# A fused encoder layer with 32 experts on one core: the order of TensorE's work in the expert pass, the third token tile as 128 rows, and the gate's activation in halves

## The reference

```
logits = xt @ w_router + b_router            # 320 tokens, 32 experts
top 4 experts of each token, gates = softmax over the 4
for each block of rows of one expert e:
    gu   = x_rows @ w_gate_up[e] + b_gate_up[e]        # 1024 -> 2048
    gate = minimum(gu[:, :1024], 7);  up = clip(gu[:, 1024:], -7, 7)
    act  = (up + 1) * gate * sigmoid(1.702 * gate)
    y    = act @ w_down[e] + b_down[e]                 # 1024 -> 1024
out[token] += gate_of_token * y
y_prompt, y_sample = rms_norm(x + out) * norm_final_g
```

## Time and profile before

| what | value |
|---|---|
| median of 3 runs | 1284.58 us (1284.41 to 1285.18) |
| the profiled execution | 1285.43 us, span 1283.7 us |
| TensorE | busy 1243.4 us, 97% |
| VectorE, ScalarE | busy 39% and 16% |
| HBM traffic | 436.33 MB, 340 GB/s over the span |
| granted TensorE clock | 0.996 |

### The profile page before, as it was taken

The page is one execution under the profiler, slowest core; times in us unless marked ns, Lnnn a source line. Parts: engine busy times, 40 slices in busy tenths (PEclk is TensorE's granted clock), DMA queues, the critical chain, the costliest instruction groups (busy, mean ns, idle before and its releaser), DMA issues.

```text
span 1283.7 us, 17240 instructions
## 1 busy us (share of the span) xinstructions
PE 1243.4 (97%) x6406; PEld 542.4 (42%) x6407; DVE 497.1 (39%) x996; ACT 207.6 (16%) x407; POOL 37.6 (3%) x64
## 2 busy tenths in 40 slices
PE   6999999999999999999999999999999999999996
PEld 5655754664333343333333334333334333333332
DVE  2643645457433333333323334233333233233334
ACT  1131224452100111001101001010011100011102
POOL 2000002400000000000000000000000000000000
PEclk9999999999999999999999999999999999999998
DMA  9623125238999969999987999996999999699995
GB/s 323 219 80 118 66 89 194 72 134 315 419 430 427 428 271 428 429 427 427 427 380 323 427 428 427 427 428 289 417 427 428 428 426 426 276 431 426 426 426 202
DMA packets 48010, 436.33 MB, mean 340 GB/s; under 512 B 6229, under 2 KB 7373, under 8 KB 19318
## 3 DMA queue, kind: packets, MB, share of 16 engines
q1 hardware_dynamic: 43984, 429.41, 80.5%
q0 software_dynamic: 2080, 6.48, 1.5%
q10 hardware_dynamic: 1926, 0.18, 0.1%
HBM read 432.33 MB, written 3.72 MB: 340 GB/s over the span
## 4 chain that ended last, share of the span: by engine, by line
PE 82%; DMA 13%; DVE 2%; issue 1%; ACT 1%; POOL 0%; ACTq 0%; SPq 0%; DVEq 0%; POOLq 0%
PE PS L1848 34%; PE PS L1888 17%; DMA ring<-in_w_gate_up_dram 12%; PE PS L1339 6%; PE PS L1348 5%; PE PS L1806 5%; PE PS L1294 4%; PE PS L1774 4%; PE PS L1350 1%; DMA dsk<-in_d_skip_dram 1%; PE PS L1642 1%; PE PS L1831 1%; PE PS L1616 1%; PE PS L1500 1%; PE PS L1503 0%
## 5 line engine op out<-in xcount | busy, mean ns | idle before, releaser
L1848 PE MATMUL PS<-ring,r 128*64 128x512 f32 x2304 | 520.0, 596 | 11.9 <-DMA ring<-in_w_gate_up_dram 11.3
L1848 PEld LDWEIGHTS PS<-ring,r 128*64 128x64 f32 x2304 | 158.6, 137 | 314.9 <-issue 281.1
L1888 PE MATMUL PS<-ring,r 128*64 128x512 f32 x1152 | 255.1, 595 | 0.3
L1163 DVE SCALAR_TENSOR_TENSOR r<-PS,gprev,r 128x512 f32<-128x512 f32 (+1 forms) x222 | 152.4, 741 | 113.6 <-PE PS L1806 112.1
L1888 PEld LDWEIGHTS PS<-ring,r 128*64 128x64 f32 x1152 | 82.2, 137 | 148.4 <-issue 146.2
L1266 DVE TENSOR_TENSOR yy<-PS,yy 128x512 fp32r<-128x512 f32 x36 | 24.9, 692 | 249.8 <-ACT yy L747 249.8
L736 ACT ACTIVATE r<-r 128x512 f32<-128x512 f32 x36 | 22.7, 629 | 504.9 <-DVE r L1249 504.9
L1249 DVE TENSOR_SCALAR r<-PS 128x512 f32<-128x512 f32 x36 | 24.9, 692 | 202.6 <-PE PS L1848 202.6
L1339 PE MATMUL PS<-r,ring 128*128 128x323 f32 x320 | 91.3, 442 | 2.1 <-ACT r L523 2.1
L1294 PE MATMUL PS<-ident,r 128*128 128x128 f32 (+5 forms) x490 | 80.6, 295 | 10.7 <-DVE r L782 9.9
L1294 PEld LDWEIGHTS PS<-ident,r 128*128 128x128 f32 (+5 forms) x490 | 61.5, 183 | 35.6 <-issue 17.6
(11 more groups left out here) (321 smaller groups left out, 742.4 us busy)
## 6 DMA issues: line engine op xcount, KB each, us to landing
ring<-in_w_gate_up_dram SPq DMA_DIRECT2D x96, 2048.0 KB, 16.3
ring<-in_w_down_dram SPq DMA_DIRECT2D x64, 2048.0 KB, 16.7
ring<-in_w_gate_up_dram SPq DMA_DIRECT2D x64, 1024.0 KB, 16.4
ring<-in_w_in_dram SPq DMA_DIRECT2D x8, 2048.0 KB, 14.8
ring<-in_w_out_dram SPq DMA_DIRECT2D x3, 2048.0 KB, 7.5
r<-in_x_prompt_dram SPq DMA_DIRECT2D x2, 512.0 KB, 3.9
r<-in_x_prompt_dram POOLq DMA_DIRECT2D x2, 512.0 KB, 4.4
out_dram<-r POOLq DMA_DIRECT2D x2, 512.0 KB, 5.5
```

Of the source, the lines that this page charges most:

```text
L1163: v.scalar_tensor_tensor(xx, PS[0:rows, out_banks(t)[h], :], gprev[0:rows, t:t + 1], xx, ALU.mult, ALU.add)\
L1848: last = mm(PS[64 * h:64 * h + 64, m, :], xt[:, k % 4, k // 4, :], w[:, kk, D * m + 512 * h:D * m + 512 * h + 512], start=False, stop=(k = ...
L1888: last = mm(PS[64 * h:64 * h + 64, 2, :], at[:, kk, c, :], w[:, kk, 512 * h:512 * h + 512], start=(c == 0 and kk == 0), stop=(c == 1 and k ...
```

## The change

Seven things are changed. On TensorE `gather` moves from behind the up products to a place ahead of chunk 3. `combine` at its old place does tile 0 alone, tiles 1 and 2 (`combine_rest`) come behind the last up product. Then follow `turn`, `places` and, last before the down products, the transposes of `ac`. The third tile of `x` holds its 64 tokens as 128 rows of 512 columns: the upper half of the columns is moved to partitions 64 to 127. Its output is one product of 128 rows for each part in place of two pairs, and one sum in place of two. The sigmoid and what feeds it and follows it run in two halves of 256 columns. The copy of bank 5 becomes four: tile 0 early, tile 1 and two blocks of 64 x 64 behind `combine_rest`. In the tail the products with the high part go ahead of the low part, into five banks. The third tile is scaled as 512 columns and written by two transfers, for which the last gain is also loaded in halves.

```
 SyncE
-            sp.dma_start(y_sample[0, :, :], xn[0:SS, 2, :]).then_inc(s["y_out"], 16)
-            sp.wait_ge(s["y_out"], 48)
+            for h in range(2):
+                sp.dma_start(y_sample[0, :, 512 * h:512 * h + 512], xn[64 * h:64 * h + 64, 2, 0:HALF]).then_inc(s["y_out"], 16)
+            sp.wait_ge(s["y_out"], 4 * 16)
 GpSimd
+            for h in range(2):
+                pool.dma_start(gfin_halves[64 * h:64 * h + 64], ... .to_broadcast([64, HALF])).then_inc(s["gfin_in"], 16)
 ScalarE
-            a.activation(place[:, 0:TC], PS[:, 4, 0:TC], ACT.Copy).then_inc(s["c_ready"], 1)
+            a.activation(place[:, 0:256], PS[:, 4, 0:256], ACT.Copy)
+            for h in range(2):
+                last = a.activation(place[64 * h:64 * h + 64, 256 + 64 * h:320 + 64 * h], PS[64 * h:64 * h + 64, 4, 256:TC], ACT.Copy)
+            last.then_inc(s["c_ready"], 1)
+            a.activation(x[64:128, 2, 0:HALF], x[0:SS, 2, HALF:D], ACT.Copy).then_inc(s["rows_split"], 1)
             def expert_pass(b):
-                act.wait_ge(s["g_ready"], b + 1)
-                a.activation(sg, ug, ACT.Sigmoid, scale=ALPHA).then_inc(s["sig_ready"], 1)
                 act.wait_ge(s["ct_mm"], b + 1)
-                act.wait_ge(s["comb_mm"], 6 * b + 6)
-                a.activation(place[:, :], PS[:, 5, 0:128 * NT], ACT.Copy).then_inc(s["c_ready"], 1)
+                act.wait_ge(s["comb_mm"], 5 * b + 2)
+                a.activation(place[:, 0:128], PS[:, 5, 0:128], ACT.Copy)
                 act.wait_ge(s["xe_mm"], b + 2)
                 a.activation(xe, bank(3), ACT.Copy).then_inc(s["xe_ev"], 1)
+                for q in range(2):
+                    part = slice(256 * q, 256 * q + 256)
+                    act.wait_ge(s["g_ready"], 2 * b + q + 1)
+                    a.activation(sg[:, part], ug[:, part], ACT.Sigmoid, scale=ALPHA).then_inc(s["sig_ready"], 1)
+                act.wait_ge(s["comb_mm"], 5 * b + 5)
+                a.activation(place[:, 128:256], PS[:, 5, 128:256], ACT.Copy)
+                for h in range(2):
+                    at0 = 256 + 64 * h
+                    last = a.activation(place[64 * h:64 * h + 64, at0:at0 + 64], PS[64 * h:64 * h + 64, 5, at0:at0 + 64], ACT.Copy)
+                last.then_inc(s["c_ready"], 1)
 VectorE
-                accumulate(6 * b, 0)
-                accumulate(6 * b, 1)
+                accumulate(5 * b, range(1), OUT_BANKS)
...
-                v.tensor_scalar(ug, bank(0), LIMIT, None, ALU.min).then_inc(s["g_ready"], 1)
-                dve.wait_ge(s["sig_ready"], b + 1)
-                v.tensor_tensor(sg, sg, ug, ALU.mult).then_inc(s["glu_ready"], 1)
+                for q in range(2):
+                    part = slice(256 * q, 256 * q + 256)
+                    v.tensor_scalar(ug[:, part], bank(0)[:, part], LIMIT, None, ALU.min).then_inc(s["g_ready"], 1)
+                for q in range(2):
+                    part = slice(256 * q, 256 * q + 256)
+                    dve.wait_ge(s["sig_ready"], 2 * b + q + 1)
+                    dve.wait_ge(s["g_ready"], 2 * b + 2)
+                    v.tensor_tensor(sg[:, part], sg[:, part], ug[:, part], ALU.mult).then_inc(s["glu_ready"], 1)
...
-                accumulate(6 * b, 2)
+                gathered(b + 1)
+                accumulate(5 * b, range(1, NT), OUT_BANKS)
...
-                gathered(b + 1)
 TensorE
+            def combine_rest(b):
+                pe.wait_ge(s["o_ev"], 5 * (b + 1) + 4)
+                for part in range(2):
+                    spread(1, part, OUT_BANKS)
+                pe.wait_ge(s["g_ready"], 2 * (b + 1) + 2)
+                for part in range(2):
+                    spread(2, part, OUT_BANKS)
+            def combine_last(b):
+                pe.wait_ge(s["c_ready"], b + 2)
+                pe.wait_ge(s["o_ev"], 5 * (b + 1) + 2)
+                for part in range(2):
+                    pe.wait_ge(s[("yy_ready", "yyl_ready")[part]], b + 2)
+                    for t in range(NT):
+                        spread(t, part, LAST_BANKS)
 in expert_pass
                     if c == outputs:
-                        combine(b - 1, 0)
-                        combine(b - 1, 1)
+                        combine(b - 1)
+                    if c == GU_CHUNKS - 1:
+                        if beside:
+                            gather_first(1)
+                        else:
+                            gather(b + 1)
...
                         last.then_inc(s["gate_mm"], 1)
-                        combine(b - 1, 2)
                         for kk in range(2):
                             last = gate_up(kk, 1)
                         last.then_inc(s["gu_mm"], 1)
-                if beside:
-                    gather_first(1)
-                else:
-                    gather(b + 1)
+                combine_rest(b - 1)
+                turn(b + 1)
+                pe.wait_ge(s["c_ready"], b + 2)
+                places(b + 1)
                 pe.wait_ge(s["act_ready"], b + 1)
                 pe.wait_ge(s["at_ev"], b + 1)
                 for c in range(4):
                     last = tr(PS[:, 4, 128 * c:128 * c + 128], every_fourth(ac, c))
                 last.then_inc(s["at_mm"], 1)
-                pe.wait_ge(s["c_ready"], b + 2)
-                places(b + 1)
-                turn(b + 1)
                 pe.wait_ge(s["at_ev"], b + 2)
-def out_banks(t):
-    return ((6, 7), (2, 4), (6, 7))[t]
+OUT_BANKS = (6, 7, 6, 7, 0)
+LAST_BANKS = (6, 7, 0, 1, 5)
```

More of the change, by code:

```diff
@@ L206, in build @@
         gfin = view(r2, 512, D)
+        gfin_halves = view(r2, 0, HALF)
         lgp = (view(r2, 1024, 128), view(r2, 1152, 128), view(r2, 1280, SS))
@@ L756, in _ @@
             a.activation(stat[:, 11:12], stat[:, 10:11], ACT.Sqrt)
[L757 to L762, removed]
+            for t in range(2):
+                act.wait_ge(s["o_ev"], 5 * total + 2 * t + 4)
+                step(a.activation(r6[:, 0:D], x[:, t, :], ACT.Square, accum_out=stat[:, t:t + 1]))
+                a.activation(stat[:, 3 + t:4 + t], stat[:, t:t + 1], ACT.Sqrt,
+                             scale=1.0 / D, bias=stat[:, 10:11]).then_inc(s["sqrt4"], 1)
+            act.wait_ge(s["o_ev"], 5 * total + 7)
+            step(a.activation(r6[:, 0:HALF], x[:, 2, 0:HALF], ACT.Square, accum_out=stat[:, 2:3]))
+            for h in range(2):
+                other = slice(64 - 64 * h, 128 - 64 * h)
+                last = a.activation(stat[64 * h:64 * h + 64, 12:13], stat[other, 2:3], ACT.Identity,
+                                    scale=1.0 / D, bias=stat[other, 10:11])
+            step(last)
+            a.activation(stat[:, 5:6], stat[:, 2:3], ACT.Sqrt, scale=1.0 / D, bias=stat[:, 12:13]).then_inc(s["sqrt4"], 1)
         @block.vector
@@ L1100, in _ @@
             add_att(3)
-            step(v.memset(place[:, TC:128 * NT].bitcast(f32), 0.0))
+            step(v.memset(place[:, 256:128 * NT].bitcast(f32), 0.0))
             step(v.memset(zeros32, 0.0))
@@ L1156, in gathered, with accumulate @@
                                 ALU.mult).then_inc(s["xt_ev"], 1)
[L1158 to L1164, removed]
+            def accumulate(n, tiles, banks):
+                for t in tiles:
+                    for h in range(2 if t < 2 else 1):
+                        dve.wait_ge(s["comb_mm"], n + 2 * t + h + 1)
+                        xx = x[:, t, 512 * h:512 * h + 512]
+                        v.scalar_tensor_tensor(xx, bank(banks[2 * t + h]), gprev[:, t:t + 1], xx, ALU.mult, ALU.add)\
+                            .then_inc(s["o_ev"], 1)
             positions_of(0, 0)
@@ L1239, in expert_pass @@
                 dve.wait_ge(s["gates_held"], b + 2)
-                accumulate(6 * b, 0)
-                accumulate(6 * b, 1)
+                if first:
+                    dve.wait_ge(s["rows_split"], 1)
+                accumulate(5 * b, range(1), OUT_BANKS)
                 dve.wait_ge(s["ct_mm"], b + 1)
@@ L1275, in _ @@
             dve.wait_ge(s["gates_held"], total + 2)
+            accumulate(5 * total, range(NT), LAST_BANKS)
+            dve.wait_ge(s["gfin_in"], 3 * 16)
             for t in range(NT):
[L1277 to L1281, removed]
                 dve.wait_ge(s["sqrt4"], t + 1)
-                step(v.reciprocal(stat[0:rows, 6 + t:7 + t], stat[0:rows, 3 + t:4 + t]))
-                v.scalar_tensor_tensor(xn[0:rows, t, :], x[0:rows, t, :], stat[0:rows, 6 + t:7 + t],
-                                       gfin[0:rows], ALU.mult, ALU.mult).then_inc(s["fin_ready"], 1)
+                step(v.reciprocal(stat[:, 6 + t:7 + t], stat[:, 3 + t:4 + t]))
+                if t < 2:
+                    v.scalar_tensor_tensor(xn[:, t, :], x[:, t, :], stat[:, 6 + t:7 + t], gfin, ALU.mult, ALU.mult)\
+                        .then_inc(s["fin_ready"], 1)
+                else:
+                    v.scalar_tensor_tensor(xn[:, t, 0:HALF], x[:, t, 0:HALF], stat[:, 6 + t:7 + t], gfin_halves, ALU.mult, ALU.mult)\
```

(32 more changed lines are left out.)

20 lines of the change are left out of this document (14 added, 6 removed).

## The result

The changed kernel takes 1304.14 us (median of 4 runs, 1303.27 to 1304.36), the one before 1284.49 us (median of 4). The ratio is 1.0149, with a 95% interval of 1.0132 to 1.0166. It is slower, as forecast, and 3.8 us above the forecast time.

The account below looks back on a forecast made before the run. TensorE's own order bounds the kernel, weights a close second. Passes 0 to 5 +5.8, cycles +5.6, last passes +5.3, tail -1.0 give +15.7 us on 1285.43, making 1301.1; less 0.85, 1300.3 us, range 1287 to 1311 (8 in 10).

Parts of the forecast that it names:

- The two waits for ScalarE: TensorE waits 0.70 us for bank 4's copy before the down products and 0.35 for `place` copies before the places.
- The pass: One pass of TensorE's work: 26.35 us plus waits of 0.70 and 0.35 makes 27.40, 0.89 longer; bounds 26.66 and 27.83.
- The copies of `place`: Three ScalarE copies behind `combine_rest` end 0.86 us after its products, seen by TensorE at 0.94; other estimate 0.65 against 0.82.
- The halves: Gate activation in two halves gains 0.7 us that nobody uses, as TensorE reaches its transposes later.
- Pass 0: First expert pass: d (0.89 us, each pass's lengthening) plus 0.5 waiting for the next block's one-hot rows; bounds 0 and 1.5.
- The cycles: Three cycles of eight passes: each from 217.35 to 219.20 us, TensorE's time above the weights' floor; +5.6 in all.
- the formula: Run's change is 12d + 0.5 - 1.0 + 3 x max(8 x pass - 217.35, -0.45); the last term is the cycles.
- the floor is about 216.9: Shortest cycle the weights allow: doubled expert's fourth chunk lands at 199.5 us, then 17.1 to the next cycle's issue.
- rival B: Weights hide it: waits total 0.7 us or less, pass at most 27.05, cycles cost nothing; +4.2, 1288.8 us; chance 0.14.
- The tail: End of the kernel: one sum fewer, high parts early, third tile on 512 columns; net -1.0 us, bounds -1.4 and -0.3.
- The gain's loads: Two added gain transfers (256 KB) take 0.6 us of DMA in a stretch without waits for weights: cost nothing.
- Rival C: Faster: one visit fewer and shorter tail win, bank 4's copy hides in the restart; -3.8, 1280.8 us; chance 0.08.

Follow-up runs that it names:

- Experiment 1: Changed kernel, only the order behind the up products altered: activation's transposes directly behind combine_rest, 1297.16 us; or places' products moved behind those transposes, 1293.21 us.
- experiment 2: Changed kernel with the gate's activation in one piece of 512 columns instead of two halves of 256: 1304.00 us.
- whole_gate: Changed kernel with one limit, one sigmoid and one product of 512 columns each in place of halves: 1304.00 us.
- places_behind: Changed kernel with the places' products, and their wait for ScalarE's copies, moved behind the activation's transposes, ahead of the down products: 1293.21 us.
- experiment 6: Kernel before plus two unused loads of the gain's halves: 1284.80 us; one_visit without those loads, ScalarE copying the halves instead: 1281.24 us.
- one_visit: Kernel before with third tile as 128 rows, its tail, gate in halves, all three tiles' outputs in one visit behind chunk 0: 1282.13 us, ratio 0.9980.
- gather_behind: Changed kernel with the gather put back behind the up products, ahead of combine_rest, ScalarE's queue order unchanged: 1391.56 us.

## Why the prediction was right, point by point

- **The direction and its cause.** The two waits for ScalarE make the pass longer, as predicted. Experiment 1 shows it: the same operations in another order give back 0.56 us a pass. The work was to be 0.16 us shorter and is only 0.02 to 0.03 shorter (26.48 us busy, 26.35 predicted).
- **The pass.** 27.40 predicted, 27.46 measured. The stop at the down products is 0.75 us (0.70), the one at the places 0.23 (0.35). `combine_rest` is 1.36 (1.22): the two products over 128 rows are 0.69 of it, so the entry that I took as 0.10 is some 0.2. The places begin 0.68 us behind it (0.94). Behind that stop they take 0.34 (0.17). The errors nearly cancel, which is luck.
- **The copies of `place`.** They start at 729.12, 729.29 and some 0.2 us later, and are done after 0.6 us, where I had 0.82 from the earlier trace rows. Those rows were a poor measure. Their copies also read a scale for each partition (`par`) and lasted 0.33 and 0.38 us each, where the copies of `place` last 0.28 and 0.21. The other estimate that the prediction gives, 0.65 us, was the nearer one.
- **The halves.** Predicted to gain nothing here, and they gain nothing (experiment 2).
- **Pass 0.** 30.79 us against 29.06 from its issue to the next, +1.7, where d + 0.5 was 1.4. TensorE waits 0.5 us for the one-hot rows, as predicted.
- **The cycles.** +8.1 against +5.6. With the pass of 27.46 the formula gives 7.0. The rest, 1.1 us, is late weights: the three cycles are 219.79, 220.03 and 220.29 us where eight passes are 219.7, and one wait of 0.39 us for chunk 2 is named. It isn't there in every execution: whole_gate has the same pass and 659.1 us for the three cycles, none late. The term that I had wrong is "the floor is about 216.9", by which nothing could be late. Its sum is wrong to begin with: from 662.24 to 680.20 are 17.96 us and not 17.5, and 199.5 + 17.1 is 216.6. And I let all of the gather hide behind the fourth chunk. It stands behind chunk 2, which lands late as well, and the fourth chunk of the doubled expert is asked for later than before (176.1 us into the cycle in places_behind, 174.4 before). The floor is 218.7 to 219.1 for 26.90 us passes. In the forecast it cost at most 1 us, but rival B was wrong by it: passes of 26.90 would not have run in 216.9. places_behind is such a kernel, and the change's formula gives it 1287.4 us. It took 1293.2.
- **The tail.** 173.55 - 168.95 - 6 x 0.95 = -1.1, predicted -1.0.
- **The gain's loads.** "Nothing" held in the changed kernel, where no weights are late in that stretch. In kernels whose pass is about as long as before they cost 1.5 us (experiment 6). The reason I gave, a stretch without waits, was no proof of slack.
- **Rival C** had one thing right: a visit less is a gain. It needs an order in which ScalarE's copies are covered, and that is one_visit.
- **The signs.** TensorE waits at the down products in all 36 passes, as the longest entry. The one sign that didn't come is a lower rate of the DMA engines: the page still has 425 to 429 GB/s in most slices of the expert stage.
- **The size.** The forecast was 15.7 us above before, the profiled execution 17.84, the medians 19.65. The expert stage alone is 19.0 us longer (6.35 + 8.1 + 4.6), 3.3 more than forecast: 0.06 us more a pass makes 2.1 of it and the late weights 1.1. That the two profiled executions differ by less is the 1.2 us ahead of the experts, which is not the change's.

## What to carry to other kernels

In an order written by hand, list for each copy by another engine what stands between its producer and its consumer on the busy engine, and keep that cover when something moves. A gain on an engine that nobody waits for (the halves here) only counts once the order has been made to need it. No wait in a stretch doesn't mean slack: two small loads turned an even race with the weights into a late one.

## What the runs showed of the hardware

- Stops of 0.23 and 0.76 us a pass leave the granted clock at 1.00 (changed kernel, 700 to 1100 us). Three stops of 0.23, 0.90 and 0.76 us within 3 us were followed by a clock of 0.53 over the next 3.6 us, which cost 1.7 us more than the stops themselves. It happened in most passes of gather_behind, not in all. In the pass whose down products begin at 803.23 us the same three stops (0.23, 0.91, 0.76) left the clock at 1.00, those products took 7.09 us and the pass 28.6 in place of 30.3. Five more passes took 28.6 to 28.7 us, and three pairs of passes took 58.8 to 58.9 in place of 60.5. What tells the two apart stays open.
- Two products over 128 rows and 512 columns take 0.66 us in one_visit behind products over 64 rows and 0.69 in the changed kernel's pass above, about as much as two pairs of 64 rows (0.66 and 0.67). Four such products behind others of their own shape took 0.92.
